# Two norm-row broadcasts wait for the gather's indices instead of for the gathered rows

## The chip, the cores and the metric

The kernel runs on one NeuronCore of a Trainium2 chip. The metric is the device time of one launch in microseconds (us), the median of several runs. The core has five engines with an instruction queue each: TensorE (PE in the profile), VectorE (DVE), ScalarE (ACT), GpSimd (POOL) and SyncE (SP). Sixteen DMA engines move data between HBM and the on-chip memory. DMAs are issued here from three queues: SP's, which streams the weights, ACT's, and POOL's, which issues the indirect ones (gathers and scatters). TensorE's clock has two levels here, 1.2 and 2.4 GHz; the profile prints the granted share, 0.50 or 1.00.

## The reference

One step of a two-layer streaming encoder over 256 prompt frames and 32 sample frames (288 tokens of 2048 numbers, fp32). Each layer is a mixer, a layer norm, a mixture of experts (MoE) and a second layer norm:

```
for i in range(DEPTH):                                  # DEPTH = 2
    mix = rg_lru_block(...) if i % 2 == 0 else pool_mixer(...)
    x = layer_norm(ALPHA * x + mix, ln_g[i, 0], ln_b[i, 0])
    ffn = hier_moe(x, ...)
    x = layer_norm(ALPHA * x + ffn, ln_g[i, 1], ln_b[i, 1])

def hier_moe(x, wg, bg, we, be, w_gate_up, w_down):
    gsel = argmax(x @ wg + bg)                          # one of 4 groups for each token
    topi = top_k(le[gsel], 2)                           # two of the 4 experts of that group
    hu = einsum('td,edf->tef', x, w_gate_up)            # 2048 x 1024 for each of 16 experts
    act = silu(hg) * hv * gates
    return einsum('tef,efd->td', act, w_down)           # 512 x 2048 for each of 16 experts
```

The weights of the two MoE stages are most of the 482 MB that the core reads.

## The kernel before

Everything is written out by hand: one instruction stream for each engine, semaphores between them, no scheduler. The stages in order of time are: the first mixer, its layer norm, MoE of layer 0, the way back to feature-major form, the second mixer, its layer norm, MoE of layer 1.

**The MoE.** Tokens are sorted into windows of 96 slots (W = 96), each window one group of four experts. A window reads 24 weight chunks of 2 MB through a ring of six slots on chip (`ring`); the SP queue issues a chunk's load as soon as PE has used up the chunk that held its slot (semaphore `parts_used`). In the first window of a layer one more chunk goes to a spare place in `xtok` (line 511), once the gathered rows are in.

**The way into a MoE**, on which the change bears, is this. ACT writes the normalised tokens in row form to `xtok`, and each of three tiles goes out to HBM as `x_rows[l]` (line 801, semaphore `x_out[l]`, full at 48). Meanwhile DVE and PE compute the routing, at whose end DVE writes the row numbers of the first window to `src_now` (line 1877, `src_ready[l]` goes to 1). POOL waits for both and issues the gather of 96 rows of 8 KB from `x_rows[l]` into `xtok[:, 0, :]` (line 578, semaphore `rows_in[l]`, full at 16 for the first window). PE keeps itself busy with 16 matmuls that nobody uses (`stay_awake(8)`, line 1114). When the rows are in, PE places them per expert (`select_rows`, line 1155), ACT and DVE copy the results to `xsel` with scale and offset (lines 834 and 1754), and PE multiplies with the gate/up weights (line 1230) and later the down weights (line 1251).

**The two broadcasts.** Work on rows needs the layer norm's gain and offset on 96 partitions. ACT's queue loads them with two DMAs of 96 x 8 KB, each reading one row of 8 KB from HBM 96 times. Their target is `ln_row`, in the memory of `xT`, the old feature-major tokens, which PE has read for the last time when the routing and the row form are done. In layer 0 they are at lines 822 and 823, in layer 1 at 825 and 826; both sit behind the two waits at lines 819 and 820. DVE's wait for them (`ln_row_in`, line 1858) stands at the second expert of the first window, ahead of line 1863. In layer 0, ACT's queue issues eight small stores of the mixer's state (line 818) just ahead of the waits.

Behind the broadcasts, ACT's next instruction is the first copy to `xsel` (line 834), which waits for PE's first placing.

Of the kernel before, what the change touches and what calls it, by code (L numbers as in the profile page):

```python
# [154 lines left out]
def encoder_step(nc, A, O):  # L155
    ctx = ExitStack()
    with ctx:
# [3 lines left out]
        def sem(name):  # L161
            return ctx.enter_context(nc.semaphore(name))
# [201 lines left out]
        src_ready = [sem(f"src_ready{i}") for i in two]  # L364
        dst_ready = [sem(f"dst_ready{i}") for i in two]
        rows_in = [sem(f"rows_in{i}") for i in two]
# [262 lines left out]
        def _(eng):  # L629
# [162 lines left out]
            def moe(l):  # L792
# [24 lines left out]
                    for j, o in enumerate(dst):  # L817
                        eng.dma_start(o.rearrange("(b p) -> b p", p=128), cstT[j:128:8, :]).then_inc(out_st, 16)
                eng.wait_ge(x_out[l], 48)
                eng.wait_ge(rows_in[l], 16)  # L820
                if l == 0:
                    for dst, name in zip(res_row[0], ("ln_g", "ln_b")):
                        eng.dma_start(dst, A[name][0, 0:1, :].to_broadcast([W, D])).then_inc(ln_row_in, 16)
# [86 lines left out]
            act_extra = []  # L910
            layer_norm(0)
            moe(0)

            for q in range(4):
# [8 lines left out]
            layer_norm(2)  # L923
            eng.wait_ge(out_st, 160)
            moe(1)
            eng.wait_ge(out_st, 160)

# [1071 lines left out]
```

## Time and profile before

| | |
|---|---|
| median of 3 runs | 1477.83 us (1476.75 to 1478.71) |
| span of the profiled execution, first to last instruction | 1473.1 us |
| PE busy | 1395.7 us (95%) |
| ACT busy | 364.8 us (25%) |
| DVE busy | 522.5 us (35%) |
| SP's DMA queue | 468.61 MB, 80.1% of the 16 engines' span |
| ACT's DMA queue | 10.27 MB, 2.2% |
| POOL's DMA queue | 8.82 MB, 1.6% |
| mean granted TensorE clock | 0.977 |

For the profiled execution only the span is given; the 4.7 us between it and the median lie before the first and after the last instruction. A row of the timeline reads: start, length, engine and line, operation, out<-in, count, and in brackets how long the engine was idle before and what it waited for. An engine's name with a q is its queue: the row is the issue of a DMA, not the transfer. In a table by stretches the columns are the stretch, its length, then busy time (and number of instructions) of PE, PEld (weight load), DVE, ACT and POOL, then the granted clock, the DMA engines' busy share and the GB/s that they moved.

### The profile page before, as it was taken

The page shows a single profiled execution, that of the slowest core. Times are in us where ns is not written, and L with a number is a line of the kernel's source. Part 1 is how long each engine was busy: PE and PEld are TensorE (multiplying, and loading weights), DVE is VectorE, ACT ScalarE, POOL GpSimd, SP SyncE. Part 2 cuts the span into 40 slices and gives each one's busy share as a digit, 9 for nine tenths or more (in the row PEclk, how much of TensorE's full clock was granted, in tenths as well). Part 3 has the DMA queues.
Part 4 walks back from the last instruction along what each step waited for, and adds up shares of the span by engine and source line. Part 5 has one row for each costly group of instructions (what it writes and reads, how often), then busy time and mean ns, then how long its engine had stood idle before and what let it go on. Part 6 is the DMA issues. An engine that isn't in the chain of part 4 may idle for free.

```text
span 1473.1 us, 20986 instructions
## 1 busy us (share of the span) xinstructions
PE 1395.7 (95%) x9148; PEld 777.5 (53%) x9148; DVE 522.5 (35%) x1079; ACT 364.8 (25%) x562; POOL 28.6 (2%) x37
## 2 busy tenths in 40 slices
PE   9999999999899999999898999899999999899895
PEld 8999999999543333243233338653343233224331
DVE  6878878543323031022002117624023013102302
ACT  5576666332300120021012002311021012002101
POOL 0000001000000000000000000000000000000000
PEclk9999999999879999999999999999999999999998
DMA  9684544744778999999999987679999999999992
GB/s 305 219 248 147 187 154 136 239 172 172 235 286 322 429 394 429 427 423 426 429 427 416 427 338 299 221 270 354 426 414 419 428 427 422 426 428 427 420 426 83
DMA packets 94567, 489.05 MB, mean 332 GB/s; under 512 B 8408, under 2 KB 64664, under 8 KB 67320
## 3 DMA queue, kind: packets, MB, share of 16 engines
q1 hardware_dynamic: 89536, 468.61, 80.1%
q10 hardware_dynamic: 2266, 10.27, 2.2%
q0 software_dynamic: 2672, 8.82, 1.6%
q8 instruction: 72, 1.18, 0.3%
q14 instruction: 21, 0.17, 0.0%
HBM read 481.95 MB, written 16.04 MB: 338 GB/s over the span
## 4 chain that ended last, share of the span: by engine, by line
PE 75%; DMA 16%; DVE 5%; issue 2%; ACT 1%; DVEq 0%; POOL 0%; ACTq 0%; POOLq 0%
PE ps L1230 21%; PE ps L1251 20%; DMA ring<-in_moe_w_down 15%; PE ps L1155 5%; PE ps L1018 5%; PE ps L1019 5%; PE ps L1020 5%; PE ps L1106 2%; PE ps L1107 2%; PE ps L1108 2%; PE ps L1179 2%; PE ps L1314 1%; PE ps L1141 1%; DMA xtok<-x_rows,src_now 1%; ACT xtok L661 1%
## 5 line engine op out<-in xcount | busy, mean ns | idle before, releaser
L1230 PE MATMUL ps<-ring,xsel 128*64 128x512 f32 x2016 | 459.8, 604 | 19.4 <-DMA ring<-in_moe_w_gate_up 18.5
L1251 PE MATMUL ps<-ring,work 128*32 128x512 f32 x3072 | 346.2, 595 | 11.3 <-DMA ring<-in_moe_w_down 11.3
L1230 PEld LDWEIGHTS ps<-ring,xsel 128*64 128x64 f32 x2016 | 137.9, 138 | 298.1 <-issue 259.6
L1251 PEld LDWEIGHTS ps<-ring,work 128*32 128x32 f32 x3072 | 91.7, 109 | 222.7 <-issue 202.7
L1841 DVE SCALAR_TENSOR_TENSOR arena<-arena,ps 64x512 f32<-64x512 f32 x32 | 21.7, 678 | 487.5 <-ACT work L874 487.5
L1018 PE MATMUL ps<-operands,whi 128*128 128x288 f32 x512 | 151.9, 297 | 0.0
L1019 PE MATMUL ps<-ring_lo,whi 128*128 128x288 f32 x512 | 151.6, 296 | 0.0
L1020 PE MATMUL ps<-operands,ring_lo 128*128 128x288 f32 x512 | 150.7, 294 | 0.0
L1387 DVE TENSOR_TENSOR ring_lo<-ring,whi 128x1024 fp32r<-128x1024 f32 x96 | 115.9, 1221 | 55.1 <-ACT whi L677 54.8
L677 ACT ACTIVATE whi<-ring 128x1024 fp32r<-128x1024 f32 x96 | 100.6, 1058 | 124.2 <-PE ps L1020 69.5
L873 ACT ACTIVATE arena<-ps 64x512 f32<-64x512 f32 x32 | 18.9, 589 | 406.3 <-PE ps L1230 406.2
L1754 DVE TENSOR_SCALAR xsel<-ps,affine_of 128x256 f32<-128x256 f32 x64 | 31.9, 540 | 228.2 <-PE ps L1155 228.2
L1018 PEld LDWEIGHTS ps<-operands,whi 128*128 128x128 f32 x512 | 97.0, 190 | 0.1
L1020 PEld LDWEIGHTS ps<-operands,ring_lo 128*128 128x128 f32 x512 | 97.0, 189 | 0.0
L1019 PEld LDWEIGHTS ps<-ring_lo,whi 128*128 128x128 f32 x512 | 96.8, 189 | 0.0
L1155 PEld LDWEIGHTS ps<-work,xtok 96*128 96x128 f32 x256 | 64.5, 326 | 47.8 <-issue 44.7
L1155 PE MATMUL ps<-work,xtok 96*128 96x256 f32 x256 | 82.2, 446 | 2.2 <-DMA xtok<-x_rows,src_now 2.2
L1106 PE MATMUL ps<-operands,whi 128*128 128x288 f32 x256 | 76.3, 298 | 2.9 <-DVE ylo L1454 2.9
L1107 PE MATMUL ps<-ylo,whi 128*128 128x288 f32 x256 | 75.5, 295 | 0.0
L834 ACT ACTIVATE xsel<-ps,affine_of 128x256 f32<-128x256 f32 x64 | 32.6, 560 | 172.7 <-PE ps L1155 172.7
L1108 PE MATMUL ps<-operands,ring_lo 128*128 128x288 f32 x256 | 75.1, 293 | 0.0
L876 ACT ACTIVATE work<-ps 128x384 f32<-128x384 f32 x32 | 15.7, 490 | 176.9 <-PE ps L1179 176.9
(348 smaller groups left out, 1223.7 us busy)
## 6 DMA issues: line engine op xcount, KB each, us to landing
ring<-in_moe_w_gate_up SPq DMA_DIRECT2D x126, 2048.0 KB, 18.2
ring<-in_moe_w_down SPq DMA_DIRECT2D x64, 2048.0 KB, 18.9
ring<-in_lru_w_in SPq DMA_DIRECT2D x15, 2048.0 KB, 10.6
ring<-in_lru_w_out SPq DMA_DIRECT2D x8, 2048.0 KB, 10.2
x_rows<-xtok ACTq DMA_DIRECT2D x4, 1024.0 KB, 3.9
xtok<-in_moe_w_gate_up SPq DMA_DIRECT2D x2, 2048.0 KB, 12.0
ring<-in_pool_w SPq DMA_DIRECT2D x4, 1024.0 KB, 14.5
xtok<-in_x_prompt SPq DMA_DIRECT2D x2, 1024.0 KB, 8.2
```

The costliest lines, as they stand in the source:

```text
L677: eng.activation(whi[:, p % NPART, :], ring_at(n)[:, at * PART:(at + 1) * PART], ACT.Copy)\
L834: last = eng.activation(xsel[:, k, :], ps[:, 6, b * 256:(b + 1) * 256], ACT.Identity, scale=affine_of[:, l, 0, k:k + 1], bias=affine_of[:, ...
L1018: mm(o, hi, yhi[:, k, :], start=(k == 0), stop=False)
L1019: mm(o, hi, xlo_block(k), start=False, stop=False)
L1020: last = mm(o, lo, yhi[:, k, :], start=False, stop=(k == KD - 1))
L1106: mm(o, hi, yhi[:, k, :], start=(k == 0), stop=False)
L1107: mm(o, hi, ylo[:, k, :], start=False, stop=False)
L1108: last = mm(o, lo, yhi[:, k, :], start=False, stop=(k == KD - 1))
L1155: last = mm(ps[:, 6 + q % 2, b * 256:(b + 1) * 256], XS.rearrange("s (c p j) -> s c j p", c=4, j=4)[:, k // 4, k % 4, :], sel[0:W, :, :].r ...
L1230: last = mm(ps[half * ES:(half + 1) * ES, e % 2, :], xsel[:, k, e * ES:(e + 1) * ES], wt[:, half * 512:(half + 1) * 512], start=(k == 0), ...
L1251: last = mm(ps[rows:rows + QB, 2 + r, :], act[:, e % 2, f * W + slots0:f * W + slots0 + QB], wt[:, d * 512:(d + 1) * 512], start=start, st ...
L1387: TT_(lo_at(n, at), ring_at(n)[:, at * PART:(at + 1) * PART], whi[:, p % NPART, :].bitcast(F32), ALU.subtract).then_inc(lo_ready, 1)
```

## The change

The second of the two waits ahead of the broadcasts asks for another semaphore. Before, it is `rows_in[l]`, which the gather raises when its rows have landed. Now it is `src_ready[l]`, which DVE raises when it has written the row numbers that the gather uses. The line serves both layers. No instruction is added, removed or put in another order on any engine.

```diff
                 eng.wait_ge(x_out[l], 48)
-                eng.wait_ge(rows_in[l], 16)
+                eng.wait_ge(src_ready[l], 1)
                 if l == 0:
                     for dst, name in zip(res_row[0], ("ln_g", "ln_b")):
                         eng.dma_start(dst, A[name][0, 0:1, :].to_broadcast([W, D])).then_inc(ln_row_in, 16)
                 if l == 1:
                     for i, name in enumerate(("ln_g", "ln_b")):
                         eng.dma_start(ln_row[i], A[name][1, 1:2, :].to_broadcast([W, D])).then_inc(ln_row_in, 16)
```

## Rows read from the trace of the kernel before

**Rows 1.** Chain that ended last, in order of time (start, us, what)
```profile
376.78 2.56 DMA x_rows<-xtok
380.24 5.68 DMA xtok<-x_rows,src_now
...
566.91 22.48 DMA ring<-in_moe_w_down
...
958.72 2.69 DMA x_rows<-xtok
962.17 5.49 DMA xtok<-x_rows,src_now
...
1136.64 23.06 DMA ring<-in_moe_w_down
```

**Rows 2.** Timeline around the gather of layer 0
```profile
378.56 0.15 DVE L1877 TENSOR_TENSOR src_now<-zn,ps 96x1 int32<-96x1 f32 x1
...
378.93 1.85 ACTq L818 DMA_DIRECT2D out_lru_conv_prompt<-cstT  x3
...
383.37 0.61 ACTq L818 DMA_DIRECT2D out_lru_h_sample<-cstT  x1
385.93 0.33 SPq L511 DMA_DIRECT2D xtok<-in_moe_w_gate_up  x1
...
385.99 0.34 ACTq L823 DMA_DIRECT2D xT<-in_ln_g  x1
386.38 0.44 ACTq L823 DMA_DIRECT2D xT<-in_ln_b  x1
387.31 1.02 ACT L834 ACTIVATE xsel<-ps,affine_of 128x256 f32<-128x256 f32 x2 [8.41 <-PE ps L1155]
```

**Rows 3.** Timeline around the gather of layer 1
```profile
960.23 0.15 DVE L1877 TENSOR_TENSOR src_now<-zn,ps 96x1 int32<-96x1 f32 x1
...
960.49 0.19 ACT L809 ACTIVATE r<-r 128x3 f32<-128x3 f32 x1
...
967.68 0.33 SPq L511 DMA_DIRECT2D xtok<-in_moe_w_gate_up  x1
...
967.70 2.25 PE L1155 MATMUL ps<-work,xtok 96*128 96x256 f32 x8 [1.70 <-DMA xtok<-x_rows,src_now]
967.74 0.34 ACTq L826 DMA_DIRECT2D xT<-in_ln_g  x1
```

**Rows 4.** Table by stretches, layer 1, around the gather and the broadcasts
```profile
966.00:967.00 1.00, 0.00 (x1) 0.00 (x0) 0.00 (x0) 0.00 (x0) 0.00 (x0) 1.00 0.41 172
967.00:968.00 1.00, 0.30 (x1) 0.30 (x2) 0.00 (x0) 0.00 (x0) 0.00 (x0) 1.00 0.02 8
968.00:969.00 1.00, 1.00 (x5) 1.00 (x6) 0.00 (x0) 0.00 (x0) 0.00 (x0) 1.00 1.00 229
...
978.00:979.00 1.00, 1.00 (x6) 0.22 (x5) 0.00 (x0) 0.00 (x0) 0.00 (x0) 1.00 0.99 229
979.00:980.00 1.00, 1.00 (x6) 0.95 (x4) 0.00 (x0) 0.00 (x0) 0.00 (x0) 1.00 0.91 213
```

**Rows 5.** Line 578, all ten gathers: issue to landing, min/median/max
```profile
DMA to landing us min/median/max: 5.5/11.1/13.0
```

**Rows 6.** Table by stretches: idle PE and the clock, both layers
```profile
374.00:377.10 3.10, 0.77 (x7) 0.58 (x6) 2.20 (x16) 2.75 (x4) 0.00 (x0) 0.97 0.82 338
...
956.00:958.80 2.80, 0.08 (x1) 0.00 (x0) 2.41 (x18) 2.69 (x4) 0.00 (x0) 0.71 0.90 374
...
960.00:964.00 4.00, 4.00 (x9) 2.86 (x10) 1.88 (x11) 0.67 (x3) 0.99 (x1) 0.50 0.28 49
964.00:966.00 2.00, 2.00 (x8) 1.23 (x7) 0.00 (x0) 0.00 (x0) 0.00 (x0) 0.99 0.34 131
...
970.20:975.00 4.80, 4.78 (x20) 2.06 (x20) 0.79 (x2) 1.02 (x2) 0.00 (x0) 1.00 0.97 328
```

**Rows 7.** Table by stretches: the same work at either clock
```profile
418.00:419.50 1.50, 0.09 (x3) 0.04 (x1) 1.50 (x4) 0.00 (x0) 0.00 (x0) 1.00 0.91 360
...
421.30:445.20 23.90, 23.90 (x84) 11.41 (x85) 2.82 (x20) 0.49 (x1) 0.00 (x0) 0.50 0.46 184
...
1000.10:1013.00 12.90, 12.87 (x84) 6.94 (x84) 1.24 (x2) 0.49 (x1) 0.00 (x0) 1.00 0.94 365
```

**Rows 8.** PE's timeline, the same matmuls in layer 0 and in layer 1
```profile
428.78 1.14 PE L1141 MATMUL ps<-vals,arena 128*96 128x10 f32 x6
431.75 1.13 PE L1141 MATMUL ps<-vals,arena 128*96 128x10 f32 x6
...
1007.70 0.68 PE L1141 MATMUL ps<-vals,arena 128*96 128x10 f32 x6
1009.32 0.68 PE L1141 MATMUL ps<-vals,arena 128*96 128x10 f32 x6
```

**Rows 9.** Table by stretches: where the weight stream runs dry, both layers
```profile
428.00:431.00 3.00, 3.00 (x12) 1.33 (x10) 0.00 (x0) 0.00 (x0) 0.00 (x0) 0.50 0.03 11
440.00:443.00 3.00, 3.00 (x12) 1.56 (x12) 1.00 (x7) 0.00 (x0) 0.00 (x0) 0.50 0.00 0
989.00:992.00 3.00, 3.00 (x13) 1.50 (x12) 0.00 (x0) 1.02 (x2) 0.00 (x0) 1.00 0.64 240
```

**Rows 10.** Timeline: first use of the rows in layer 0, dense matmuls in layer 1
```profile
450.54 2.28 DVE L1863 SCALAR_TENSOR_TENSOR xtok<-xtok,xT 96x2048 f32<-96x2048 f32 x1
...
992.11 3.65 PE L1230 MATMUL ps<-ring,xsel 128*64 128x512 f32 x16
```

## The prediction, made before the changed kernel had run

> **What bounds the kernel now.** I read the chain that ended last first, then the timelines around both places where the changed wait stands, then tables by stretches of the DMA engines and of the clock.
>
> The chain runs through the gather in both layers: the last store of token rows lands at 376.78 + 2.56 = 379.34 us and 958.72 + 2.69 = 961.41, POOL's gather is issued at 380.24 and 962.17 and has landed 5.68 and 5.49 us later, and PE goes on from there [rows 1]. A microsecond that the gather loses is at first lost to the end. The chain names waits for weights only from 566.91 and 1136.64 on [rows 1]. The question is whether the weight stream has slack ahead of these that could swallow a delay or pass on a saving. It runs dry in between: the DMA engines' share is 0.03 at 428 to 431 and 0.00 at 440 to 443 in layer 0, and 0.64 at 989 to 992 in layer 1 [rows 9]. There the ring is full and the next load waits for PE to free a slot. So what the DMA engines gain before those points is lost again in the idle stretch, and what PE loses before them delays every later load by as much. The path to price is gather, PE, end.
>
> **Part 1, the wait taken away.** It never held anything that matters. ACT issued the broadcasts at 385.99 and 386.38, done at 386.82, and its next work, the first copy to xsel, started at 387.31 because PE's placing ended then [rows 2]. Gain: 0. DVE's first reading of the rows is at 450.54 in layer 0 [rows 10], 64 us after the issue. Gain: 0. In layer 1 the same pair of rows is needed later still. If this cover were gone, an earlier landing would be worth what the broadcasts come early, 2 and 6 us.
>
> **Part 2, when the broadcasts go out now.** The row numbers are written at 378.71 and 960.38 [rows 2, 3], before the last store has landed, so ACT is released by that store, or by its own queue.
> Layer 0: ACT's queue is issuing eight small stores until 383.37 + 0.61 = 383.98 [rows 2]. The broadcasts go out at 384.0 instead of 385.99, 2.0 us earlier.
> Layer 1: nothing is in the way, ACT's last activation ends at 960.68 [rows 3], and the last store lands at 961.41. The broadcasts go out at about 961.5 instead of 967.74 [rows 3], 6.3 us earlier and ahead of the gather's issue at 962.17.
> Both DMAs and their 16 engines are the same as before; only their neighbour changes. Before, it was the spare weight chunk (issued 385.93 and 967.68 [rows 2, 3]), for which nobody waited; now it is the gather, for which PE waits.
>
> **Part 3, the gather beside the broadcasts, layer 1.** The two broadcasts are 2 x 96 x 8 KB = 1.57 MB. They are slow for their size: at 978 to 980, where the engines are 0.99 and 0.91 busy, they move 229 and 213 GB/s [rows 4]. At 221 GB/s they take 7.1 us. A load's bytes come about 1 us after its issue (spare chunk: issued at 967.68 [rows 3], 8 GB/s until 968, 229 GB/s after it [rows 4]), so they would have the engines from 962.5 to 969.6. The gather's 0.79 MB moved until 967 [rows 4]. The trace shows no gather beside a broadcast, so I bound it:
> - lower bound 0: the gather alone leaves the engines half idle (share 0.41 at 966 to 967 [rows 4]), and its rows might fit into the gaps. I exclude a gain, since nothing leaves the gather's time.
> - upper bound: among weight loads a gather takes 11.1 us in the median and 13.0 at most, against 5.5 alone [rows 5], so +5.6 to +7.5. But the broadcasts are a finite 1.57 MB. If they all go first, until 969.6, and the gather's rows follow in some 3 us, it lands at about 973, +5.3.
> - between: both queues take turns row by row. From 964, when the gather's rows start, they and an equal 0.79 MB of broadcast have to move, 1.57 MB at the 328 GB/s of the mixed stretch 970 to 975 [rows 6]: 4.8 us, to 968.8, where the gather alone was done at about 967. That is +1.8. The weight loads delay a gather by more than such a turn-taking explains, so I go above it.
> I take **+2.7 us**, nearer to the turn-taking, because what is queued ahead is short.
>
> The Trainium skill has a rule for and one against. "DMA: Bandwidth & Descriptors", section "Rules for kernel authors", says to issue a DMA early and wait late, which would make this change free; section "Issuing engines are not separate DMA queues" of the same page says that DMAs from different engines run on the same 16 engines and interleave. By the first the sum would stay 0, by the second it is the +1.8 or more. The 11.1 us against 5.5 of the gathers [rows 5] is on the side of the second.
>
> **Part 4, the same in layer 0.** Issued at 384.0, the first bytes come at about 385, behind the eight small stores of the same queue; the gather has landed at 385.92 [rows 1]. Bounds 0 and +0.9 (all that is left of it then). I take +0.1.
>
> **Part 5, TensorE's clock in layer 1.** The stay-awake matmuls end at 966.0; PE then idles 1.70 us until the gathered rows are in [rows 3, 4], with the clock at 1.00. With the gather 2.7 us later the idle time is 4.4 us. What the rows show of such gaps: 3.10 us with 0.77 busy (2.3 idle) and 2.80 us with 0.08 busy (2.7 idle) each ended with the clock falling to 0.50 [rows 6]; in 960 to 964 it is still 0.50, and it is back at 0.99 from 964 on [rows 6], some 7 us at half clock. So I expect a fall at 4.4 us idle. Its price: 23.9 us at 0.50 in layer 0 hold the work that takes 12.9 us (x84 matmuls in both) at 1.00 in layer 1 [rows 7], 46% of the half-clock time lost. A fall of 7 us costs 0.46 x 7 = 3.2 us. Bounds: 0 if it doesn't fall; if it doesn't come back before the dense matmuls at 992.11 [rows 10], all of 970.4 to 992 runs at half clock, where a group of matmuls that repeats every 1.62 us takes 2.97 [rows 8], so 21.7 x 0.83 = 18 us. I take 3.2, since the work after the gap is dense (4.78 of 4.80 us busy [rows 6]) like that which ended the 7 us falls.
>
> **The sum.** 0 (part 1) + 0.1 (part 4) + 2.7 (part 3) + 3.2 (part 5) = +6.0 us. Against the profiled execution's span: 1473.1 + 6.0 = 1479.1; with the 4.7 us outside it, the median goes from 1477.83 to **1483.8 us**.
>
> **The rivals.**
> *A, late gather, clock holds.* The clock stayed at 1.00 over the gap of 1.70 us. It decides at a delay of about 0.7 us, where the gap would reach the 2.3 us that fell. Time: 1477.83 + 0.1 + 0.6 to 2.7 = 1478.5 to 1480.7.
> *B, late gather, clock down for long.* For it speaks layer 0, where it stayed down 23.9 us though PE was 23.90 busy [rows 7]. Time: 1477.8 + 2.8 + 8 to 18 = 1489 to 1499.
> *C, the change does nothing.* The gather's rows fit into the gaps of the engines, or the queue serves it first. Time: 1477.8, within 0.5.
> *D, faster: a fall of the clock in layer 0 goes away.* PE was idle at 418.0 to 419.5 (0.09 busy), and the clock then stayed at 0.50 for 23.9 us; in layer 1 the same work kept 1.00 [rows 7]. This is close to an edge, and a shift of layer 0's PE work by some tenths (part 4 reaching 0.5 us or more) could tip it. It would give back 23.9 - 12.9 = 11.0 us: 1477.8 - 11.0 = 1466.8 alone, 1472.8 beside my forecast. Against it: part 4 is near 0.
> *E, faster: the weight stream counts.* The 1.57 MB of broadcasts leave the stretch behind each gather, up to 7.1 us of the engines' time in each layer. If the end hung on the stream from there, the time would be 1477.8 - 7.1 + 2.8 = 1473.5. Against it stand the idle stretches of the engines, above all the 0.00 at 440 to 443 [rows 9].
>
> **How the numbers follow.** My forecast (late by 2 to 4 us, a short fall) 0.45, at 1481 to 1488; A 0.19; B 0.14; C 0.12; D 0.06; E 0.04. The range leaves out D, E and the upper half of B: **1477 to 1494**. About 0.2% (3 us) is what a measurement of this kernel can tell from no change. Slower by more than that: the forecast 0.45, B 0.14, and a part of A 0.05, together 0.64. Same: the rest of A and C, 0.26. Faster: D and E, 0.10.
>
> **What would show it.** In the changed kernel's timeline: the issue of the broadcasts at about 384.0 and 961.5 (part 2); the gather of layer 1 landing 8.2 us after its issue instead of 5.49, that of layer 0 within 0.2 of 5.68 (parts 3 and 4); PE's idle time ahead of its first placing in layer 1 at 4.4 us, and a granted clock of 0.50 for some microseconds behind it (part 5); from there on all rows of layer 1 shifted by one amount, with the engines idle longer around 989 (the path). It is wrong if the gather of layer 1 lands in under 6 us, if the clock holds or stays down past 980, or if the long fall in layer 0, from 421.30 on, is gone.

## The result, and the profile after

The change makes the kernel slower. The median of 17 runs is 1483.3 us (1468.75 to 1488.13), that of 17 runs of the kernel before beside it 1475.48 us (1462.16 to 1479.36). The ratio is 1.0073, with a 95% interval of 1.0048 to 1.0099. The predicted time was 1483.8 us.

The times of both kernels fall into two groups, with a gap between. Of the kernel before, 5 runs lie at 1462 to 1465 us (median 1463.9, called short here) and 12 at 1472 to 1480 (median 1476.6, called long); of the changed one 2 lie at 1468.75 and 1472.37 (middle 1470.6) and 15 at 1480 to 1489 (median 1483.5). Like compared with like, the change costs 6.7 and 6.9 us. The gap is the long fall of the clock in layer 0: the mean granted clock of the changed kernel's two short runs is 0.982 and 0.980 and that of its long ones 0.968 to 0.974, the trace of one short run (experiment 3) has no such fall, and experiments 4 and 6 take it away. Since the kernel before happened to have more of the short runs, the ratio of all (0.73%, 10.8 us) overstates the change; 6.9 of 1476.6 us is 0.47%.

The chain that ended last, around both gathers, in the changed kernel (start, us, what); it answers to [rows 1]:

```profile
384.36 5.51 DMA xtok<-x_rows,src_now
...
962.18 2.66 DMA x_rows<-xtok
...
965.60 9.62 DMA xtok<-x_rows,src_now
975.22 0.04 issue
975.26 3.80 PE ps L1155 x8
```

Layer 0's gather takes 5.51 us from issue to landing (5.68 before), layer 1's 9.62 (5.49 before). Layer 1's gather is issued at 965.60 instead of 962.17, 3.43 us later; of this nothing comes from the change, since at layer 0's gather the kernel was already 4.12 us late (384.36 against 380.24) and no changed instruction had run. Some 0.8 us of it are there by 22 us into the launch. The other 3 us came at 268 to 275 us, in the first mixer, where the same matmuls had the full clock in the execution before and half of it in this one:

```profile
267.78:274.60 6.82, 6.82 (x54) 6.79 (x54) 5.93 (x12) 1.96 (x2) 0.00 (x0) 1.00 1.10 349
```

```profile
267.78:274.60 6.82, 6.82 (x30) 6.50 (x29) 5.55 (x12) 1.06 (x1) 0.00 (x0) 0.50 1.10 350
```

The first block is the kernel before, the second the changed one (columns as in [rows 4]: the share behind the five engines is the clock).

The timeline of the changed kernel around layer 1's gather, which answers to [rows 3]:

```profile
963.69 0.15 DVE L1877 TENSOR_TENSOR src_now<-zn,ps 96x1 int32<-96x1 f32 x1
...
964.86 0.34 ACTq L826 DMA_DIRECT2D xT<-in_ln_g  x1
...
965.23 0.45 ACTq L826 DMA_DIRECT2D xT<-in_ln_b  x1
...
965.60 0.99 POOL L578 DMA_INDIRECT xtok<-x_rows,src_now  x1 [142.06 <-DMA x_rows<-xtok]
975.24 0.33 SPq L511 DMA_DIRECT2D xtok<-in_moe_w_gate_up  x1
...
975.26 3.80 PE L1155 MATMUL ps<-work,xtok 96*128 96x256 f32 x8 [5.79 <-DMA xtok<-x_rows,src_now]
```

The broadcasts go out 0.74 and 0.37 us before the gather. What the DMA engines do meanwhile stands in the table by stretches (columns as in [rows 4]; the last three are clock, DMA share and GB/s):

```profile
966.00:967.00 1.00, 1.00 (x3) 0.71 (x3) 0.00 (x0) 0.00 (x0) 0.59 (x1) 0.50 1.00 311
967.00:968.00 1.00, 1.00 (x4) 0.75 (x4) 0.00 (x0) 0.00 (x0) 0.00 (x0) 0.74 1.03 246
...
970.00:971.00 1.00, 0.00 (x0) 0.00 (x0) 0.00 (x0) 0.00 (x0) 0.00 (x0) 1.00 1.02 246
971.00:972.00 1.00, 0.00 (x0) 0.00 (x0) 0.00 (x0) 0.00 (x0) 0.00 (x0) 1.00 0.90 230
972.00:973.00 1.00, 0.00 (x0) 0.00 (x0) 0.00 (x0) 0.00 (x0) 0.00 (x0) 1.00 0.41 131
973.00:974.00 1.00, 0.00 (x0) 0.00 (x0) 0.00 (x0) 0.00 (x0) 0.00 (x0) 1.00 0.55 229
974.00:975.00 1.00, 0.00 (x0) 0.00 (x0) 0.00 (x0) 0.00 (x0) 0.00 (x0) 0.67 0.18 74
```

From 966 to 972 the engines are full (share about 1) and move only 230 to 311 GB/s, the mark of the broadcasts [rows 4]. From 972 to 975 comes the picture of a gather alone: a share of 0.2 to 0.55. The two hardly mix. The packets of the trace say it in full: the broadcasts' rows start 0.25 to 6.09 us after the gather's issue and the last one ends at 6.62; the gather's rows start 6.16 to 8.76 us after its issue, where they start 1.68 to 4.88 us after it in the kernel before.

PE meanwhile idles 5.79 us, and the clock falls. The same table, over longer stretches:

```profile
974.40:981.10 6.70, 5.84 (x14) 3.31 (x16) 1.00 (x2) 1.02 (x2) 0.00 (x0) 0.50 0.74 262
981.10:990.00 8.90, 8.90 (x38) 4.50 (x34) 1.00 (x2) 1.02 (x2) 0.00 (x0) 1.00 0.53 184
998.00:1001.00 3.00, 3.00 (x13) 1.39 (x13) 0.00 (x0) 1.02 (x2) 0.00 (x0) 1.00 0.41 175
```

The last row shows the weight stream dry, as 989 to 992 was before [rows 9], with a share of 0.41 instead of 0.64. The time that the broadcasts no longer take from the stream is idle there.

In layer 0 the queue order was as foreseen (answers to [rows 2]):

```profile
387.49 0.61 ACTq L818 DMA_DIRECT2D out_lru_h_sample<-cstT  x1
388.19 0.53 ACTq L823 DMA_DIRECT2D xT<-in_ln_g  x1
388.76 0.59 ACTq L823 DMA_DIRECT2D xT<-in_ln_b  x1
389.89 0.33 SPq L511 DMA_DIRECT2D xtok<-in_moe_w_gate_up  x1
```

ACT issued the broadcasts 3.83 us after the gather's issue, 1.7 before its landing, and their first row moved when the gather's last had gone (5.26 against 5.22 us after the issue).

### The profile page after: what moved, and what is told of

Same layout as the page of the kernel before. It is cut to its first block, busy times and chain, and to the rows that moved or that the text cites. A ratio compares the mean times of both kernels' runs of the same rounds, so it can differ in the third digit from the quotient of the medians.

```text
span 1484.2 us, 20986 instructions
## 1 busy us (share of the span) xinstructions
PE 1401.6 (94%) x9148; PEld 780.6 (53%) x9148; DVE 522.6 (35%) x1079; ACT 365.2 (25%) x562; POOL 28.6 (2%) x37
## 4 chain that ended last, share of the span: by engine, by line
PE 74%; DMA 17%; DVE 5%; issue 2%; ACT 1%; DVEq 0%; POOL 0%; SPq 0%; ACTq 0%; POOLq 0%
PE ps L1230 21%; PE ps L1251 20%; DMA ring<-in_moe_w_down 14%; PE ps L1155 5%; PE ps L1018 5%; PE ps L1019 5%; PE ps L1020 5%; PE ps L1106 2%; PE ps L1107 2%; PE ps L1108 2%; PE ps L1179 2%; PE ps L1314 1%; DMA xtok<-x_rows,src_now 1%; DMA ring<-in_lru_w_in 1%; PE ps L1141 1%
## 5 line engine op out<-in xcount | busy, mean ns | idle before, releaser
L1251 PE MATMUL ps<-ring,work 128*32 128x512 f32 x3072 | 346.2, 595 | 10.5 <-DMA ring<-in_moe_w_down 10.5
## 6 DMA issues: line engine op xcount, KB each, us to landing
xtok<-in_moe_w_gate_up SPq DMA_DIRECT2D x2, 2048.0 KB, 10.4
```

The lines of the kernel that those rows point to most:

```text
L1251: last = mm(ps[rows:rows + QB, 2 + r, :], act[:, e % 2, f * W + slots0:f * W + slots0 + QB], wt[:, d * 512:(d + 1) * 512], start=start, st ...
```

## The experiments

Where a place in a trace decides, it is given beside the time, since a single time can be 12 us off by layer 0's clock. "Long" and "short" runs are those with and without the long fall in layer 0.

**1. Layer 1 alone, and 2. layer 0 alone.** The changed wait in one layer only:

```diff
-                eng.wait_ge(rows_in[l], 16)
+                if l == 1:                      # in experiment 2: l == 0
+                    eng.wait_ge(src_ready[l], 1)
+                else:
+                    eng.wait_ge(rows_in[l], 16)
```

> Only layer 1's broadcasts wait for the row numbers; layer 0's wait for the gathered rows as before. Theory (the loss is all in layer 1: 4.1 us of gather and 2.9 us of clock): gather of layer 1 lands about 9.6 us after its issue, PE idles over 5 us ahead of its first placing, the clock falls to 0.50 for some 7 us behind it, time 7 us above the kernel before. Rival (both layers share the loss): less than 5 us above it. The long fall of the clock in layer 0 comes and goes from run to run and moves a single time by 11 us, so the trace's places decide before the time does.

> Only layer 0's broadcasts wait for the row numbers. Theory: ACT's queue is held by the eight small stores until the gather is nearly done, so the gather of layer 0 lands 5.5 to 5.7 us after its issue and the time stays within 0.5 us of the kernel before at the same state of layer 0's clock. Rival (the shift tips layer 0's clock): the fall behind the idle place at 418 to 419.5 us is gone or longer in most runs, the time 11 us lower or some us higher.

Layer 1 alone: median 1480.67 us of 10 runs against 1473.71 of 35, ratio 1.0047 (1.0009 to 1.0085). Long runs 1481.4 against 1475.1, short ones 1470.8 against 1463.0: +6.3 and +7.7. Its chain has layer 1's gather at 10 us:

```profile
963.55 10.04 DMA xtok<-x_rows,src_now
```

PE idled 6.25 us and the clock fell from 972.2 to 979.0. Layer 0 alone: median 1475.56 us, ratio 1.0010 (0.9978 to 1.0042), nine long runs at 1475.9 and one short at 1463.6, +0.8 and +0.6. Layer 0's gather in the chain of this kernel:

```profile
381.59 5.66 DMA xtok<-x_rows,src_now
```

So the loss is in layer 1. In layer 0 nothing can be told from no change, though I had expected within 0.5 us; the rival, that the shift tips layer 0's clock, is not seen (9 long runs of 10, against 26 of 35 before). Layer 0's gather is not always spared, though. With the changed wait there it took 5.5 to 5.8 us in the traces of this experiment, of the changed kernel and of experiments 5a and 6, but 6.62 us in that of experiment 3, where the first eight rows of the broadcasts moved ahead of its last one. What that cost at the end is not measured.

**3. PE kept awake in layer 1.** On top of the change:

```diff
-                stay_awake(8)
+                stay_awake(8 if l == 0 else 20)
```

> The changed kernel with 40 instead of 16 stay-awake matmuls in layer 1, so that PE is busy until the late gather has landed. Theory (idle PE is what makes the clock fall): the gather of layer 1 still lands about 9.6 us after its issue, but no fall of the clock follows it, and the stretch from landing to the dense matmuls takes 24.4 us as in the kernel before; time 4.1 us above the kernel before, 2.9 below the changed one. Rival (the clock falls for another reason, such as the load on the DMA engines): the fall at about 974 us stays and the time is 7 us above.

The timeline of this kernel around layer 1's gather:

```profile
954.16 0.99 POOL L578 DMA_INDIRECT xtok<-x_rows,src_now  x1 [142.12 <-DMA x_rows<-xtok]
964.09 0.33 SPq L511 DMA_DIRECT2D xtok<-in_moe_w_gate_up  x1
...
964.12 2.25 PE L1155 MATMUL ps<-work,xtok 96*128 96x256 f32 x8 [0.26 <-DMA xtok<-x_rows,src_now]
```

And its table by stretches, behind the gather:

```profile
964.00:974.00 10.00, 9.62 (x38) 5.38 (x38) 1.99 (x4) 2.04 (x4) 0.00 (x0) 1.00 0.75 244
```

The gather still takes 9.9 us, PE idles 0.26 us, and the clock holds at 1.00 behind it, with the DMA engines about as busy ahead of it as in the changed kernel (share 0.73 at 956.2 to 964.0). That idle PE is what makes the clock fall is borne out in the trace, and so is the price of the fall. The dense matmuls of [rows 10] come here:

```profile
988.52 3.65 PE L1230 MATMUL ps<-ring,xsel 128*64 128x512 f32 x16
```

From PE's first placing to them it is 24.40 us, as before (967.70 to 992.11, 24.41); in the changed kernel it is 26.68 (975.26 to 1001.94), 2.27 more. The times (median 1474.13, ratio 1.0021, 0.9983 to 1.0059) don't settle the sum: five short runs at 1468.4 are 5.4 us above the short ones of before, five long ones at 1481.1 are 6.0 above the long ones. Experiment 6 repeats it without layer 0's fall.

**4. The idle place in layer 0 filled.** In the kernel before, six unused matmuls where PE waits for the places of the later windows:

```diff
                         if first and PLACES_AT <= i < PLACES_AT + WINS:
                             if i == PLACES_AT:
+                                if l == 0:
+                                    stay_awake(3)
                                 eng.wait_ge(P_ready, 2 * l + 2)
```

> The kernel before with six stay-awake matmuls (about 1.5 us) in layer 0 where PE idles at 418.0 to 419.5 us. Theory (that idle place is what makes the clock fall for 24 us): the clock holds from 421 to 445 us, the same work takes 13 instead of 24 us, and the time is near 1464 us in nearly all runs, where the kernel before has it in 5 of 17. Rival (the fall comes from the thin work behind it, not from the idle place): the fall stays, and the time is as before within 1 us.

All 12 runs lie at 1462.7 to 1466.2 us, median 1464.72, ratio 0.9945 (0.9919 to 0.9972). The table by stretches answers to [rows 7]:

```profile
417.50:419.10 1.60, 1.60 (x10) 1.17 (x8) 1.60 (x4) 0.00 (x0) 0.00 (x0) 1.00 1.06 420
419.10:432.00 12.90, 12.90 (x85) 6.96 (x84) 1.10 (x2) 0.49 (x1) 0.00 (x0) 1.00 0.89 336
```

PE is busy through the former gap, and x85 matmuls take 12.9 us at full clock, where x84 took 23.9 at half. The fall behind the idle 1.4 us costs 11.0 us by these rows; by the times, 10.4 us lie between the long runs and this kernel, and 12.1 between the long and the short runs of the kernel before, which has 26 long ones of 35. The idle time alone does not decide it. In the changed kernel PE idles 1.41 us there and the clock falls:

```profile
422.00:424.00 2.00, 0.59 (x7) 0.58 (x6) 1.97 (x5) 0.00 (x0) 0.00 (x0) 1.00 0.98 410
424.80:448.60 23.80, 23.80 (x82) 11.56 (x82) 2.06 (x15) 0.49 (x1) 0.00 (x0) 0.50 0.47 184
```

In the profiled execution of experiment 3, a short run, it idles the same 1.41 us (in the first of these stretches) and the clock holds:

```profile
420.00:432.00 12.00, 10.59 (x66) 5.21 (x62) 4.09 (x15) 0.49 (x1) 0.00 (x0) 1.00 0.90 355
432.00:440.00 8.00, 8.00 (x48) 3.49 (x46) 3.23 (x23) 0.00 (x0) 0.00 (x0) 1.00 0.58 236
```

What decides in a launch is not shown; without the idle place all 12 runs are short.

**5. What the gather waits for.** Four kernels, one run each, read from their traces. In the first only the first broadcast goes early, the second waits for the rows. In the second the broadcasts wait for a mark that POOL sets behind the issue of the gather. In the third the broadcasts are as before and the spare weight chunk of SP goes early. The fourth is the change with the chunk early as well. They are called 5a to 5d here; 5b and 5c are edits of the kernel before, 5a and 5d of the changed one.

```diff
# 5b, broadcasts behind the gather's issue
                 fetch(1)
+                eng.memset(mark[0:1, 0:32], 0.0).then_inc(gather_sent, 1)
...
-                eng.wait_ge(rows_in[l], 16)
+                eng.wait_ge(gather_sent, l + 1)
# 5c and 5d, the spare chunk early (SP)
-                            eng.wait_ge(rows_in[l], 16)
+                            eng.wait_ge(x_out[l], 48)
+                            eng.wait_ge(src_ready[l], 1)
```

> As the changed kernel, but only the first broadcast (0.79 MB) goes out early; the second waits for the gathered rows. In the changed kernel the gather's first row of layer 1 was moved only when the last row of the broadcasts had gone. Theory (what is queued ahead goes first, whole): the first broadcast is gone about 3.5 us after its first row, so the gather lands some 6.2 to 6.6 us after its issue instead of 9.6 (5.5 without a broadcast ahead). Rival (turn-taking, 1 to 1): both halves of the broadcasts cost in proportion, so it lands at about 7.6 us.

> The broadcasts wait for a mark that POOL sets right behind the issue of the gather, about 1 us after the gather's start and 4 us before its rows are in. Theory (order of arrival): the gather's rows are queued ahead, so it lands 5.5 to 6.5 us after its issue and the clock in layer 1 holds; time as the kernel before. Rival (the engines prefer ACT's queue to POOL's, whatever came first): it lands later than 8 us.

> The kernel before, with the broadcasts waiting for the rows, but the spare weight chunk (2.1 MB, SP's queue) issued when the row numbers are out. Theory (any transfer that is queued ahead delays the gather by its own length, whoever issues it): the chunk takes some 4.9 us at 430 GB/s and is gone about 5 us after the gather's issue, so the gather lands 8 to 8.5 us after it in both layers. Rival (it is the broadcasts' own pattern, 96 readings of one row, that blocks the gather): it lands within 6.5 us.

> The changed kernel with the spare chunk early too: 3.7 MB in two queues ahead of layer 1's gather. Theory (all that is queued ahead goes first): the gather's first row is moved some 11 us after its issue and it lands at 13 to 14 us. Rival (an engine takes only a limited number of rows ahead and then takes turns, as the ten gathers among weight loads suggest, with 11.1 us in the median): it lands at 10 to 12 us, with its rows moved while the other queues still move theirs.

The gather of layer 1 in the chains of the four, in this order, each block from another kernel:

```profile
962.38 6.89 DMA xtok<-x_rows,src_now
```

```profile
962.01 7.05 DMA xtok<-x_rows,src_now
```

```profile
969.29 9.28 DMA xtok<-x_rows,src_now
```

```profile
970.63 17.26 DMA xtok<-x_rows,src_now
```

From the packets of layer 1, in us after the gather's issue (of the gather the start of its first and last row, of the others the start of the first and the end of the last; "after" is behind the landing):

| | gather's rows | broadcasts' rows | chunk | landing | PE idle |
|---|---|---|---|---|---|
| before | 1.68 to 4.88 | after | after | 5.49 | 1.70 |
| change | 6.16 to 8.76 | 0.25 to 6.62 | after | 9.62 | 5.79 |
| 5a, one early | 3.43 to 6.06 | from 0.24, second after | after | 6.89 | 2.92 |
| 5b, behind the issue | 1.68 to 5.52 | 3.29 to 13.15 | after | 7.05 | 3.28 |
| 5c, chunk early | 4.30 to 8.63 | after | 0.20 to 7.10 | 9.28 | 5.49 |
| 5d, all early | 5.27 to 15.37 | 1.37 to 16.79 | 0.22 to 11.83 | 17.26 | 13.52 |

Three things follow.

It is not the broadcasts' own pattern: the chunk delays the gather by 3.8 us, nearly as much as the broadcasts (5c, landing later than the 8 to 8.5 I gave it), and in layer 0 it lands 9.65 us after its issue.

What is ahead goes first only up to a point. With one broadcast ahead (5a) the gather's first row again moves only when the broadcast's last one starts (3.43 against 3.40), and it lands at 6.89, a little behind the 6.2 to 6.6 of the theory and ahead of the rival's 7.6. But in 5d its first row moves at 5.27, with both other queues still moving for 6.6 and 11.5 us, so the theory that all that is queued goes first is wrong, and so is the rival's price of 10 to 12 us: the gather's rows move in groups of eight, and at first 1.6 us apart (from 5.3, 6.9 and 8.6 us) instead of 0.5 (from 6.2, 6.7 and 7.1) as in the changed kernel.

And the order of issue helps (5b), but does not save the gather: its rows start as early as in the kernel before, yet 42 rows of the broadcasts start among them, and it lands 1.6 us late, between the 5.5 to 6.5 of the theory and the 8 of the rival. So a gather that is issued first is not moved whole, and ACT's queue is not always preferred. Whether all rows of the gather were in the queue when the broadcasts came, the trace does not say, and so why the queues mix here and not in the changed kernel stays open.

The times of the single runs are 1476.28, 1478.25, 1488.84 and 1495.19 us, against 1473.77 of the kernel before beside them. All four traces have the long fall in layer 0, and the run before has the clock of a long one (0.975), so they may be compared: 2.5, 4.5, 15.1 and 21.4 us more. The first two are within the spread of the long runs of the kernel before (1471.9 to 1479.7). In 5c and 5d both layers' gathers are late.

5a and 5b also show falls of the clock behind shorter idle times: with 2.92 and 3.28 us it fell in both, from 971.5 to 974.9 and from 970.7 to 974.1. The row of 5b's table by stretches:

```profile
969.20:974.00 4.80, 4.80 (x14) 2.64 (x16) 0.99 (x2) 1.02 (x2) 0.00 (x0) 0.66 1.04 239
```

**6. The change without layer 0's fall.** All with the six matmuls of experiment 4 and measured beside each other: that kernel again, the change on top, and the change with the 40 stay-awake matmuls of experiment 3.

> The kernel before with the six extra matmuls in layer 0, once more, as the base for the next two: with the long fall of the clock gone, a price of a few microseconds can be read from times. Theory: 1463 to 1466 us in every run. Rival (its narrow spread was chance): some runs near 1475.

> The changed kernel with the same six matmuls in layer 0. Theory (the change costs the gather 4.1 us and the clock 2.3 to 2.9 us, in layer 1 alone): 6.4 to 7.0 us above the fill-alone kernel, in every run. Rival (the change costs only the 4.1 us of the gather, the rest was the state of layer 0's clock): 4 to 5 us above it.

> The same with 40 stay-awake matmuls in layer 1 ahead of the late gather. Theory (the clock's part is what idle PE costs, the gather's part stays): 4.1 us above the fill-alone kernel, 2.3 to 2.9 below the change with the fill. Rival (the extra matmuls cost as much as the clock gives back, as the earlier pair of runs left possible with +5.4 instead of 4.1): no lower than the change with the fill.

| | runs | median | lowest to highest |
|---|---|---|---|
| fill alone | 10 | 1462.84 | 1461.14 to 1466.5 |
| fill alone, with experiment 4 | 22 | 1463.68 | 1461.14 to 1466.5 |
| change and fill | 10 | 1470.57 | 1468.09 to 1472.01 |
| change, fill and awake | 10 | 1468.48 | 1466.48 to 1472.36 |

The ranges of the first and the third row don't touch. The change costs 7.7 us against the 10 runs beside it and 6.9 against all 22; keeping PE awake gives back 2.1 of it. There the ranges overlap, but in 81 of the 100 pairs of runs the kernel kept awake is the faster one. The gather in the chain of the change with the fill:

```profile
952.08 10.00 DMA xtok<-x_rows,src_now
```

The same kernel's table by stretches, the fall of the clock:

```profile
960.60:967.60 7.00, 5.48 (x14) 3.13 (x16) 1.00 (x2) 1.02 (x2) 0.00 (x0) 0.51 0.69 245
```

The kernel with 40 stay-awake matmuls, the same place:

```profile
962.00:970.00 8.00, 7.74 (x32) 4.42 (x31) 0.99 (x2) 2.04 (x4) 0.00 (x0) 1.00 0.69 262
```

The rival, that the extra matmuls cost what the clock gives back, falls: 2.1 us remain, a little under the 2.3 to 2.9 that I gave. With the clock held, 4.8 us are left over the 22 runs (5.6 over the 10), where I expected 4.1. The trace accounts for 4.5 of them: the gather took 9.8 us (from 952.50 to SP's next issue at 962.26, which waits for it) against 5.47 in the fill-alone kernel, and the 40 matmuls held PE 0.2 us longer, until 962.47. The rest is not explained.

## Why the prediction was right

**The path.** The chain gather, PE, end was read rightly up to the second half of layer 1. Of the profiled execution's 11.1 us over the span of before (1484.2 against 1473.1), 3.43 were there ahead of layer 1's gather, then 4.13 from the gather. The clock is read off the dense matmuls of [rows 10], which start at 992.11 before and here:

```profile
1001.94 1.51 PE L1230 MATMUL ps<-ring,xsel 128*64 128x512 f32 x6
```

That is 9.83 us later; less 3.43 and 4.13, the clock took 2.27. The shift stays at 9.83 until 1079.2, where PE waits 0.57 us for a chunk of down weights, which it did not do before; then it is 10.5. From the next windows on, where the weights are the limit [rows 1], it is no longer one amount: 12.3 at 1150, 11.3 at 1273, 12.9 behind a fall near 1380 that lasts 6.8 us instead of 3.4, and 11.1 at the end. These steps I did not follow up; they may belong to the launch and not to the change.

**Part 1, no gain.** Right, though in layer 1 the rows are not needed "later still": DVE first reads them at 1028.6 in the kernel before, 61 us after their issue, against 64 in layer 0. The earlier landing of the broadcasts shows nowhere, and the relief of the weight stream went into longer idle engines at 998 to 1001.

**Part 2, times of issue.** Right to 0.1 us in layer 1 (0.74 us ahead of the gather, foreseen 0.7), and in layer 0 the eight stores held ACT's queue until the gather was 3.7 us under way.

**Part 3, the gather in layer 1.** The mechanism was right, the term was too small: +4.13 us in the profiled run, +4.5 in experiments 1 and 6, against +2.7. The step that failed is the choice of value. I took it near the turn-taking (+1.8) with the reason that "what is queued ahead is short". The traces show the opposite end of the range: a short queue goes ahead almost whole, and the bound "if they all go first" (+5.3) was the nearer row. Turn-taking exists too, but it is seen only behind the head start (5d) or where the gather is issued first (5b).

The turn-taking term was also mis-sized. The gather does not move 96 rows: the indices of empty slots are left out, and the packets show 61 rows of 8 KB in layer 1 and 56 in layer 0, in every trace. With 0.50 MB instead of 0.79, the same working gives 1.0 MB at 328 GB/s, 3.0 us from 964, and so a landing no later than before. With the right size, turn-taking stood for about +0 and not for +1.8, so it was even further from the measured +4.1. In the bound "if they all go first" the broadcasts took 6.4 us instead of 7.1, which is most of why +4.1 came and not +5.3.

By the Trainium skill, page "DMA: Bandwidth & Descriptors", section "Queues, rings and completion order", each DMA engine goes round between its queues packet by packet. Experiment 5d agrees from 5.3 us on, when all three queues move rows. In its first five us, and in the changed kernel, the gather gets no turn; whether its rows were already queued then, the traces do not show.

**Part 4, layer 0.** Foreseen +0.1, measured 5.51 us against 5.68 in the profiled run, and 5.66 in experiment 2. Right for these; in the trace of experiment 3 the delay was 0.9, the upper bound.

**Part 5, the clock.** A fall of some 7 us was foreseen and one of 6.8 came (974.3 to 981.2), in the changed kernel and in experiments 1 and 6. Its price was 2.27 us instead of 3.2. The rate of 46% came from 23.9 us in which PE was busy throughout; here the fall began 0.9 us before PE started again, and 5.9 us of it met work: 2.27 of 5.9 is 38%. Why the rate is lower in that part is not shown.

**The sum.** +6.0 foreseen, 6.7 to 6.9 measured between like runs. The two errors, 1.4 to 1.8 too little for the gather and 0.9 too much for the clock, partly cancel. The median agrees to 0.5 us, which is luck to a part: the base itself moved from 1477.83, the median of three long runs, to 1475.48 with more of them, and 15 of the changed kernel's 17 runs were long too. Nor do 4.7 us lie outside the span: runs whose time and span are both known differ by 1.7 to 2.2 us. The profiled execution was thus one of about 1475.2 us, and the other 2.6 us were the distance to the median of three.

**The rivals.** A (clock holds) did not come about, since the idle time was 5.8 us. B (clock down for long) did not either; the clock was back after 6.8 us. C and E are out by the traces. D named the right edge in layer 0, and experiment 4 shows it to be worth about the 11.0 us I gave it (10.4 by the times); but it tips from launch to launch in the kernel before too, and the change is not seen to tip it (2 short runs of 17 here, 3 of 10 in experiment 1 and 5 of 10 in experiment 3, against 5 of 17 and 9 of 35, are too few to tell).

## What to carry to other kernels

A wait that seems to hold nothing up may be what keeps a transfer off the engines while a shorter and more urgent one is on them; before moving a DMA earlier, list what is in flight then and who waits for it. A DMA with a later need should be issued when the urgent one has landed, not merely behind its issue. And where PE stands idle even for 1.4 us, look at the granted clock behind it, in more than one execution: six unused matmuls in such a gap gave 0.55% here.

## What the runs showed of the hardware

- Two DMAs of 96 x 8 KB that read one row of HBM 96 times move 246 to 262 GB/s with all 16 engines full (967 to 971 in the changed kernel), where weight loads move 420 to 430. They take 6.4 us for 1.57 MB.
- A gather of 61 rows issued 0.7 us behind such a pair moved its first row 6.2 us after its issue instead of 1.7; behind a weight chunk 4.3 us after it; behind both 5.3 us after it, and then only 10 us of turns brought it home (17.3 us in all).
- Where PE waits for a gather, the clock fell at idle times of 2.92, 3.28, 4.6 (layer 0 in 5c), 5.0 (layer 0 in 5d), 5.5, 5.8, 6.3 and 13.5 us (5d), and not at 0.26, 1.53 (layer 0 in experiment 3) and 1.70. The fall lasted 3.4 us in the first two cases, 10.2 and 13.7 in the two of 5d, and 6.8 in the others.
- Behind the idle 1.41 us in layer 0, with small matmuls between the large ones after it, the clock fell for 23.9 us in some launches and held in others. With the idle place filled it held in all 22 runs, as far as their times tell.
